# Where GpSimd issues the token gather in the expert stage: in front of its two weight splits, or between them

## The reference

```
gates = one_hot(group) * within * g_top                 # top-1 group, top-2 experts in it
for e in range(16):
    he = silu(t @ w1[e]) * (t @ w3[e])                  # w1, w3: 1024 x 256
    y += gates[:, e] * (he @ w2[e])                     # w2: 256 x 1024
```

## Time and profile before

| | us |
|---|---|
| median of 3 runs | 1198.0 (1196.94 to 1200.09) |
| the profiled execution, its own time | 1200.9 |
| its span in the profile | 1199.0 |
| PE busy | 1067.9 (89%) |
| DVE busy | 697.8 (58%) |
| ACT busy | 524.5 (44%) |
| POOL busy | 343.2 (29%) |
| DMA below<-in_w in the chain of waits | 8% of the span |

### The profile page before, as it was taken

The page is one execution under the profiler, slowest core; times in us unless marked ns, Lnnn a source line. Parts: engine busy times, 40 slices in busy tenths (PEclk is TensorE's granted clock), DMA queues, the critical chain, the costliest instruction groups (busy, mean ns, idle before and its releaser), DMA issues.

```text
span 1199.0 us, 18236 instructions
## 1 busy us (share of the span) xinstructions
PE 1067.9 (89%) x5777; PEld 862.4 (72%) x5777; DVE 697.8 (58%) x1326; ACT 524.5 (44%) x1025; POOL 343.2 (29%) x368
## 2 busy tenths in 40 slices
PE   5999999999988899999999999975899999999950
PEld 4889889985555677777778787863777787877840
DVE  4330610117766667576565655448767777777867
ACT  4432421213532333323333333313777787888823
POOL 3100510000541111111110101102665565656755
PEclk9999999999888899999999999986999999999985
DMA  8340141122579586565555444825988787877677
GB/s 279 110 163 1 45 142 48 50 83 57 198 273 357 197 303 242 192 232 214 208 198 199 156 171 143 305 117 166 323 294 301 247 281 244 287 245 255 257 239 275
DMA packets 105764, 242.83 MB, mean 203 GB/s; under 512 B 15248, under 2 KB 63840, under 8 KB 95456
## 3 DMA queue, kind: packets, MB, share of 16 engines
q1 hardware_dynamic: 81312, 117.42, 28.9%
q0 software_dynamic: 23328, 122.17, 28.7%
q10 hardware_dynamic: 1056, 2.36, 0.6%
HBM read 243.31 MB, written 48.94 MB: 244 GB/s over the span
## 4 chain that ended last, share of the span: by engine, by line
PE 58%; DMA 13%; DVE 9%; issue 7%; SPq 5%; ACT 5%; POOL 2%; POOLq 0%; ACTq 0%; DVEq 0%
DMA below<-in_w 8%; PE ps L1078 4%; PE ps L2196 4%; PE ps L2197 4%; PE ps L2198 4%; PE ps L931 4%; PE ps L949 3%; SPq L1428 3%; PE ps L1119 3%; PE ps L1027 3%; PE ps L1120 3%; PE ps L2191 3%; PE ps L2190 3%; PE ps L2192 3%; PE ps L1123 3%
## 5 line engine op out<-in xcount | busy, mean ns | idle before, releaser
L1846 DVE TENSOR_TENSOR low<-below,high 128x1024 fp32r<-128x1024 f32 x128 | 157.0, 1260 | 36.6 <-ACT high L1543 36.2
L1642 PE MATMUL ps<-high 128*128 128x512 f32 x384 | 155.7, 406 | 11.2 <-DVE low L1856 7.4
L1518 POOL TENSOR_TENSOR low<-below,high 128x1024 fp32r<-128x1024 f32 x62 | 127.9, 2064 | 95.7 <-ACT high L1563 94.7
L1644 PE MATMUL ps<-high,low 128*128 128x512 f32 x384 | 150.8, 393 | 0.0
L1643 PE MATMUL ps<-low,high 128*128 128x512 f32 x384 | 150.6, 392 | 0.0
L1543 ACT ACTIVATE high<-below 128x1024 fp32r<-128x1024 f32 x128 | 130.4, 1069 | 41.5 <-DMA below<-in_w 41.3
L655 ACT ACTIVATE arena<-ps 128x512 f32<-128x512 f32 (+8 forms) x100 | 50.1, 510 | 170.6 <-PE ps L931 170.2
L931 PE MATMUL ps<-arena 128*128 128x128 f32 (+4 forms) x613 | 93.3, 274 | 7.8 <-ACT arena L655 2.2
L799 POOL DMA_DIRECT2D high<-wo_dram x34 | 18.6, 548 | 280.1 <-PE ps L1123 269.2
L1642 PEld LDWEIGHTS ps<-high 128*128 128x128 f32 x384 | 72.6, 189 | 28.3 <-issue 11.6
L949 PE MATMUL ps<-arena 128*128 128x64 f32 (+2 forms) x624 | 82.9, 268 | 6.9 <-DVE arena L704 2.9
(11 more groups left out here) (251 smaller groups left out, 2224.7 us busy)
## 6 DMA issues: line engine op xcount, KB each, us to landing
below<-in_w SPq DMA_DIRECT2D x256, 256.0 KB
high<-wo_dram POOLq DMA_DIRECT2D x36, 1024.0 KB, 6.0
low<-wo_dram POOLq DMA_DIRECT2D x36, 1024.0 KB, 8.4
below<-in_w POOLq DMA_DIRECT2D x64, 512.0 KB
y_dram<-arena SPq DMA_DIRECT2D x32, 512.0 KB, 5.7
arena<-in_x_prompt SPq DMA_DIRECT2D x15, 512.0 KB
below<-in_w_in SPq DMA_DIRECT2D x14, 512.0 KB, 7.7
out<-arena SPq DMA_DIRECT2D x9, 512.0 KB, 2.7
```

What stands on the lines that cost most here:

```text
L1518: pool.tensor_tensor(w2_lo[s % UN][:, c], w2_in[:, c], w2_hi[s % UN][:, c].bitcast(F32), ALU.subtract).then_inc(s_w2lo, 1)
L1642: pe.matmul(out, x_hi, w_hi, start=start, stop=False)
L1644: return pe.matmul(out, x_lo, w_hi, start=False, stop=stop)
L1846: dve.tensor_tensor(chunk(w13_lo[j], c), chunk(w13_in, c), chunk(w13_hi[j], c).bitcast(F32), ALU.subtract).then_inc(s_w13lo, 1)
```

## The change

In `moe_pool`, the gather of the slot two ahead is issued between the two splits of the second weights, and no longer in front of the first. Nothing is added or removed.

```diff
         for s in range(SLOT_TILES):
-            if s + UN < SLOT_TILES:
-                gather(s + UN)
             if s == SLOT_TILES - 2:
                 fetch_first(range(SOON))
             if s + 1 < SLOT_TILES:
                 for c in range(2):
+                    if c and s + UN < SLOT_TILES:
+                        gather(s + UN)
                     pool.wait_ge(s_w2hi, 2 * s + c + 1)
                     pool.tensor_tensor(w2_lo[s % UN][:, c], ...).then_inc(s_w2lo, 1)
                 load_second(s + 1)
```

## The result

The changed kernel takes 1224.15 us (median of 4 runs, 1216.9 to 1228.76) against 1197.9 us: ratio 1.0199, 95% interval 1.0165 to 1.0233, so slower by 1.7 to 2.3%. The profiled execution is the shortest of the four: 1216.9 us, span 1215.0. A second set (5 runs) gave 1228.8.

What follows compares the result with a forecast made beforehand. DMA engines full and POOL's chain in the full stretch, SP's loads and result copy in the alternate, PE in the last. 7.0 + 3.4 + 2.7 = 13.1 us on 1198.0 gives 1211, range 1196 to 1227 (own 1203 to 1219).

Steps and rivals of the forecast that it cites:

- rival 1: POOL's queue: w2 has to wait behind the moved gather and lands later; 28 us slower, 1226; chance 0.20.
- Rivals 2 and 4: Absorbed by shorter landings, 1199.5; or nothing changes since POOL waits for ACT between its splits anyway; together chance 0.17.
- one of three: Signs of error: no PE wait at L1653; full-stretch laps still 11.8 us; SP's last load landing under 6.3 us.
- Rival 3: Alternate stretch: faster by shorter landing of w1 and w3, with turn under 1.3 us late; 6 us, 1192; chance 0.13.
- Full stretch: Where nearly every slot brings a new expert: load of w2 1.75 us later, four laps, 7.0 us (0 to 18).
- The 1.75 us for the gather on POOL: One moved gather between POOL's two splits: 1.35 us mean plus issue, delaying load of w2 up to 1.75 us.
- rival 2: Full DMA engines return the delay as shorter landing, alternate stretch stays inside its lap; 1199.5; chance 0.17 with the do-nothing rival.
- Alternate stretch: Where every second slot brings a new expert: lap 20.2 us against 19.85, nine laps, 3.4 us (0 to 17).
- the bound of 17: Alternate stretch's upper bound: w2 landing at 966.3 and gather taking 8 us give 21.7 a lap, 17 us.
- The gather that I costed at nothing: Alternate stretch: other gather of each pair, moved into the pause, issued 4.9 us before its turn; costed at nothing.
- Last stretch: From 1110 on, all slots with the last expert, PE the bound: late gather counts whole; 2.7 us (0 to 4).
- the gather that I named: Last stretch: issued at 1114.65, landing at 1123.4 for a turn at 1120.73, while nine residual tiles load; 2.7 us.

Runs made afterwards that it cites:

- e5: Kernel before, with POOL's sequencer reading the experts once more ahead of each load of w2, so only the load goes out later: 1213.85 us, ratio 1.0110.
- e2: Kernel before, with POOL writing 128x1024 zeros between the two splits (slots 0 to 25), gather as before: 1214.75 us, ratio 1.0143.
- e7: Changed kernel, with POOL's second split doing only 448 of its 1024 columns from slot 2 on: 1222.89 us, ratio 1.0181.
- the second profile: Profile of the changed kernel run again without any edit, of its longest execution: 1228.79 us, ratio 1.0230; also called the repeat.
- e11: Kernel before, with the gather moved between the splits only from slot 26 on: 1206.18 us, ratio 1.0040.
- e3: Changed kernel, with the gather moved in front of the first split but behind that split's wait for ACT: 1214.08 us, ratio 1.0133.
- e6: Kernel before, with one more POOL subtraction of 128x1024 behind the gather in every second slot from 9 to 25: 1231.91 us, ratio 1.0175.
- e4: Kernel before, with the first half of the next slot's w2 loaded between the two splits: 1217.06 us, ratio 1.0139.

## Why the prediction was right, and where it was wrong

- *Sign and mechanism.* Slower by more than 0.3% was given 0.70, the range 1196 to 1227 held 1224.15. PE waits in front of L1653 for the gather in every second slot of the alternate stretch, 1.9 us on the mean there, where "2 us late" was written. The median lies outside the forecast's own range (1203 to 1219) and nearer to rival 1 (1226) than to the forecast (1211). That nearness is in part luck: rival 1 adds 11 + 14.6 + 2.7 us, the first profile has 6.9 + 6.6 + 4.6, and most of what the second has beyond it is the clock, which neither had. Rivals 2 and 4 are out.
- *A sign of being wrong that came true.* "SP's last load lands in under 6.3 us" was one of three; it landed in 4.9 to 6.3 us in the first profile (5.7 to 8.0 in the second), 5.5 on the mean for 6.9. Rival 3 was right on this half: with the gathers moved, w1 and w3 do land sooner. Its other condition, the turn less than 1.3 us late, failed in every second slot, where the turn was 1.4 to 2.3 us late, and so the lap got longer and not shorter.
- *Full stretch: right size, mostly another cause.* 7.0 us forecast, 6.9 and 7.6 measured. Two laps of the chain through POOL took 865.60 - 852.51 = 13.1 and 910.31 - 897.40 = 12.9 us, where 11.8 was before and 13.5 forecast. The 1.75 us for the gather on POOL were too many: most take 0.99 us with 0.15 to 0.17 ahead. And "I take 7.0, because the chain names the load's issue" doesn't hold as the main cause: with only the load late the stretch lost 2.3 us (e5, 4.0 at equal clock) and with only POOL time added 2.2 (e2); with the gather late and the splits short 8.3 (e7). More than half of the 11.8 us of the lap was the landing of w2 in full DMA engines, and a later load got part of its delay back, as rival 2 said: 4.79 us at 865.60 where it was 5.72. What cost more was the gather, which I had not costed here at all: PE waited for seven of them, at 858.04 for 2.74 us, at 892.24 for 2.52, 11 us together.
- *Alternate stretch: right parts, two sizes too small.* The load went out 6.0 us behind the start of the first split for 5.6 forecast; the first split took 2.92 us and not 2.1, beside DVE. It landed in 5.4 us for 4.1, and the second gather in 6.7 for 5.5; its landing lies between rows 9 and rows 8. The lap came to 20.9, not 20.2, the stretch to 6.6 us, not 3.4 (and to 18.1 in the second profile, over the bound of 17). The gather that I costed at nothing was in time. The Trainium skill (DMA: Bandwidth & Descriptors, section "Queues, rings and completion order") says, of the queues of SyncE and ScalarE, that each DMA engine takes descriptors in ring order. If POOL's queue does the same, w2 stands behind the gather; the trace agrees in part, since w2 takes 1.8 us longer to land, while the gather ahead of it was through by 964.1.
- *Not in the sum: the clock.* A pause of about 2.3 us can be followed by 3 us at 1.2 GHz, 1.6 us a time. That is nothing in the alternate stretch of the first profile and 8.5 us in the repeat, and so a large part of the way from 1217 to 1229.
- *Last stretch.* 2.7 us forecast with a bound of 4, 4.6 measured, and in the first profile not for the gather that I named. The one before it, for the turn at 1125.12, was 2.37 us late, and a lower clock behind it cost 1.6 more; the gather of the residual tiles (landing 8.5 us) then found PE late already and was in time by 1.7 us. In the second profile and in e11 it was the one that I named: PE waited 3.59 and 3.46 us for it.
- *Two terms taken as additive that are not.* In the alternate stretch a late gather with the load behind it (e7: +9.7), a late load alone (e5: +7.4) and both with collisions (changed kernel: +6.6) cost about the same. I read this as several rings of waits that close within about 1 us of each other in the kernel before, so that whichever grows sets the lap; no run shows that directly. In the changed kernel the chain goes through the gather, and SP's longer landing, by which e5 lost its time, isn't there (4.9 to 6.3 us for 7.4 to 8.4). That speaks for the gather as the cause of the 6.6 us; how much a gather in time would have saved, with the load still late, can't be told from these runs, since e3, which had that, lost 8.9 with collisions. That the collisions of the changed kernel's DVE splits (1.43 us for 1.26) cost anything beyond the rest isn't shown: e7 is as slow without them.

## What to carry to other kernels

A prefetch that looks five us early may have no room: write down for each the time from its new issue to its use, and set the landing times of the busiest moments against it, not the median. Ask also what else is moving when a shifted load moves: in e5 another queue's loads took about 1 us longer each time. On an in-order engine, place what others wait for from far away in front of its waits and not behind them. And where several rings of waits close within a few per cent of each other, even an edit that starts a load earlier can break the fit; measure such an edit alone before explaining it.

## What the runs showed of the hardware that I had not expected

- DVE and GpSimd slow each other in subtractions on SBUF operands. A DVE split of 128x1024 takes 1.23 us alone; three of them took 7.65 us beside POOL's subtractions, and two of POOL's took 5.53 us instead of 4.18 (e6). In e4 four of DVE's took 5.65 us for 4.82, and one of POOL's 3.02 for 2.0.
- The same pause of TensorE, 2.34 us, was followed by a lower clock in one execution (0.63 us for a matmul of 0.40) and by none in another.
- Where a load of 1 MB on POOL's queue went out 1.56 us behind its usual place, the last of SP's loads took about 1 us longer to land (e5: 7.4 to 8.4 us; before: 6.7 to 7.1).
